# The decay matrix of a gated DeltaNet branch, with the constant triangle as stationary operand, in a one-core decoder layer

## The chip, the cores and the metric

The kernel runs on one core of one Trainium2 chip. The metric is device time in microseconds (us), median over runs. The core has a TensorE (PE in the profile; PEld is its loading of stationary operands), a VectorE (DVE), a ScalarE (ACT), a GpSimd (POOL) and a SyncE (SP), which issues all DMAs of this kernel.

## What is computed

One decoder layer over 512 positions of width 1024: three branches (differential attention with 8 heads, a gated DeltaNet with 8 heads, cross-attention into 256 memory tokens) read one normalised input through one wide projection, are gated, merged and projected; a squared-ReLU MLP follows. The change touches the DeltaNet branch, of which this much matters:

```python
g = -jnp.exp(dn_a_log[l]) * jax.nn.softplus(dn_a + dn_dt_bias[l])
G = jnp.cumsum(g, axis=-1)
decay = jnp.exp(jnp.where(causal, G[..., :, None] - G[..., None, :], -jnp.inf))
lower = jnp.where(strict, jnp.einsum('bhnid,bhnjd->bhnij', k_beta, k) * decay, 0.0)
intra = jnp.where(causal, jnp.einsum('bhnid,bhnjd->bhnij', q, k) * decay, 0.0)
```

The kernel works with chunks of 128 positions. For one head and chunk the exponent of the decay is a sum of g over the positions t that come after j and up to i. Written as a matrix product that is the sum over t of AFTER[t, j] * UPTO[t, i] * g[t], where AFTER and UPTO are constant 0/1 triangles. The g can be multiplied into either triangle before the product.

## The kernel before, in words

Two stages. The **mixing stage** (to about 760 us with the branches, to about 965 us with the last gate tiles and the merge) multiplies 104 tiles of weight columns with the normalised input. A tile is 128 columns of the combined projection; its product with all 512 positions goes to one of two PSUM banks (`acc`). Each float32 product is made of three fp32r products (L1866 to L1868: high by high, high by low, low by high), 8 x 3 matmuls of 512 columns for a tile. For each tile ScalarE casts the weights to their high part (L1066, `w_hi`), VectorE subtracts for the low part (L1388, `w_lo`), and ScalarE copies the finished bank out (`evac`). Three tiles of weights are held split ahead. The second stage (merge, output projection, MLP) is untouched by the change.

Between the eighths of the main tiles TensorE does the **side steps** of the branches, in a plan that `plan_order` makes when the kernel is built: a list of steps for each engine from a table of durations (`PE_US`, `ACT_US`, `DVE_US`, `POOL_US`), dependencies, and the order of the tiles in `ORDER`. The first 12 half tiles follow a table of their own (`first_order`). All engines work off their lists strictly in order; the plan decides places only, and semaphores hold the true dependencies.

The side steps of the DeltaNet run for four pairs of heads, p = 0 to 3, so 8 blocks (2 heads x 4 chunks) at a time, with results in `ps_d`, three PSUM banks that all these steps share:

- `dk` transposes k (L2009); ScalarE squares and copies it (L1209, L1210), VectorE makes the norms and `k_fac` (L1594 to L1601), GpSimd multiplies AFTER with the decays of 8 blocks into `d_ET` (L994).
- `dE` multiplies `d_ET` with UPTO, 8 float32 matmuls of 128 columns (L2016). ScalarE takes exp (L1207), GpSimd multiplies with `k_fac` (L999).
- `dq`, `dv` transpose q and v; VectorE writes V (L1604). `dL`, `dA` are the products of k with k and with q (L2051), multiplied by `d_ET` on VectorE (L1607, L1611).
- `T1`, `Za`, `Wb`, `Z5`, `W5`, `Zl`, `Wl` invert the triangular matrix with many 32x32 matmuls (L2023, L2027, L2029), `dU`, `dW`, `sa`, `sb`, `dO` apply it and carry the state.

The attention side steps are `av`, `as0`, `as1`, `at`, `ap`, `ay` for each head (L1970 to L1990). `as0` of head 0 is the first to use the bias strip, to which VectorE adds the causal mask (L1531).

The decays g themselves (`gdec`) come from VectorE's routine `beta_and_decay` (L1461 to L1483), which raises `g_ready`; the PE step `decay` (L2073) waits for it. In the list of VectorE a conv tile is four instructions (`conv`: L1493 and three of L1495), then ScalarE's tanh (L1155) and VectorE's product (L1510). A main tile t may start on TensorE when its low part is there (`lo_ready`) and tile t-2 is copied out (`acc_free`):

```python
if k0 == 0:
    pe.wait_ge(lo_ready, t + 1)
    pe.wait_ge(acc_free, t - 1)
```

In the stretch where the first `dE` stands, tiles 0 to 7 are `dk0 dk1 dq0 dq1 dv0 dv1 dz0 dz1`.

Of the kernel before, what the change touches and what calls it, by code (L numbers as in the profile page):

```python
# [23 lines left out]
F32R = mybir.dt.float32r  # L24
I32 = mybir.dt.int32
ALU = mybir.AluOpType
# [29 lines left out]
NCONST = 4 + NM  # L56

# [15 lines left out]
PE_US = {"dE": 1.79, "dL": 1.79, "dA": 1.79, "dU": 1.79, "dW": 1.79, "T1": 0.55, "Za": 0.55, "Wb": 1.05, "Z5": 0.55, "W5": 0.9, "Zl": 1.2, "Wl": 1.2, "sa": 0.45,  # L73
# [5 lines left out]
POOL_US = {"dk": 2.4, "dE": 2.4, "dL": 2.5, "dA": 5.8}  # L79
# [9 lines left out]
         ("gate", 1), ("head", 1), ("conv", 2), ("head", 2), ("gate", 1), ("z", 1), ("head", 3), ("gate", 2), ("z", 2),  # L89
         ("head", 4), ("gate", 2), ("conv", 3), ("head", 5), ("gate", 5), ("head", 6), ("head", 7), ("gate", 4),  # L90
         ("z", 3), ("gate", 9)]
# [335 lines left out]
def build(nc, weights, x, mem, w_ba, params, consts, onehot, relb, post_g, y_dram, gate_dram, f_dram, frep_dram, out):  # L427
# [18 lines left out]
    with ExitStack() as ctx:  # L446
# [17 lines left out]
        cst = sb("cst", [P, NCONST, P])  # L464
# [39 lines left out]
        names = ["U", "SCR", "K", "KB", "V", "TF", "XB", "ET", "LT", "AT", "TT"]  # L504
        B = {n: sd_("d_" + n, [P, 8, P]) for n in names}
        U, SCR, K, KB, V, TF, XB, ET, LT, AT, TT = (B[n] for n in names)
# [12 lines left out]
        eyes = cst[:, C_MASK0 + NM - 1, 0:QB]  # L519
# [180 lines left out]

        LAMS, LAME, NLAM = smd[:, 2:4], smd[:, 4:6], smd[:, 6:7]
# [143 lines left out]
        def _(sp):  # L845
# [25 lines left out]
            sp.dma_start(cst[:, C_ID + 1:], consts[:, C_ID + 1:]).then_inc(in_cst, 16)  # L871
# [103 lines left out]
        def _(pool):  # L975
# [8 lines left out]
            def delta(i):  # L984
# [5 lines left out]
                if kind == "dk":  # L990
                    pool.wait_ge(g_ready, 1)
                    if p:
                        pool.wait_ge(yb_out, 16 * p)
                    last = nc.gpsimd.tensor_tensor(ET[:], over(cst[:, C_AFTER, :], 8),  # L994
                                                   along(flat(gdec[:, heads]), P), ALU.mult)
# [365 lines left out]
        def _(dve):  # L1361
# [97 lines left out]
            def beta_and_decay():  # L1459
# [4 lines left out]
                dve.wait_ge(in_cst, 16)  # L1464
# [12 lines left out]
                for n in range(15, 1, -2):  # L1477
# [5 lines left out]
                V_.scalar_tensor_tensor(out=gdec[:], in0=ba[:, 1], scalar=-1.0, in1=along(ealog, ST),  # L1483
                                        op0=ALU.mult, op1=ALU.mult).then_inc(g_ready, 1)
# [34 lines left out]
            def attn(i):  # L1519
# [8 lines left out]
                else:  # L1528
                    if (kind, h) == ("as0", 0):
                        dve.wait_ge(strip_in, 16)  # L1530
                        link(V_.tensor_tensor(strip[:, :, P:2 * P], strip[:, :, P:2 * P],  # L1531
                                              over(cst[:, C_CAUS, :], HA), ALU.add))
# [271 lines left out]
        def _(pe):  # L1804
# [188 lines left out]
            def delta(i):  # L1993
# [20 lines left out]
                elif kind == "dE":  # L2014
                    for m in range(8):
                        last = mm(dst[m], ET[:, m], cst[:, C_UPTO, :], start=True, stop=True)  # L2016
# [50 lines left out]
            def decay():  # L2067

                pe.wait_ge(g_ready, 1)
                pe.wait_ge(in_cst, 16)  # L2070
# [286 lines left out]
```

## Time and profile before

| | |
|---|---|
| median of 3 runs | 1351.75 us (1351.54 to 1351.91) |
| profiled execution: time | 1350.3 us |
| profiled execution: span, first to last instruction | 1348.5 us |
| TensorE busy | 1322.5 us, 98% of the span |
| VectorE, ScalarE, GpSimd busy | 753.9, 470.9, 191.5 us |
| mean granted TensorE clock | 0.995 of full |

The profiled execution is one run with the profiler on; its own time is 1.8 us above its span. Busy times of TensorE count overlapping, pipelined matmuls once. A row of a timeline gives an instruction's start and its duration with pipeline fill; what a matmul costs in a stream is the distance between starts.

### The profile page before, as it was taken

How to read it: one execution, taken by the hardware profiler on the slowest of the kernel's cores; microseconds unless marked ns; L12 is line 12 of the kernel's file. 1: busy time of each engine (PE TensorE's matmuls, PEld its weight loads, DVE VectorE, ACT ScalarE, POOL GpSimd, SP SyncE). 2: the span in 40 equal slices, each digit the busy share in tenths (PEclk: the TensorE clock that was granted, in tenths of full speed). 3: DMA queues.
4: the chain of work that ended last, by engine and by line, in shares of the span. 5: the costliest groups of instructions: out<-in, count | busy, mean ns of one | idle time of the engine just before them, and what ended most of it. 6: DMA issues, size and time to landing. Idle time of an engine off the chain costs nothing.

```text
span 1348.5 us, 24282 instructions
## 1 busy us (share of the span) xinstructions
PE 1322.5 (98%) x10413; PEld 1111.1 (82%) x10413; DVE 753.9 (56%) x1289; ACT 470.9 (35%) x779; POOL 191.5 (14%) x136
## 2 busy tenths in 40 slices
PE   9899999999999999999999999999989999999997
PEld 8689987787788887888788888888988888888786
DVE  6885253675776675677447534554466522355335
ACT  5353424433443444334243421213443222222220
POOL 1113000012000130003101042233112200022000
PEclk9999999999999999999999999999999999999999
DMA  6064313232213222222213466654323333332311
GB/s 222 28 203 139 100 48 110 78 95 72 72 48 94 94 72 88 66 99 92 83 48 102 141 210 211 191 161 132 128 92 111 106 112 94 94 94 95 109 63 63
DMA packets 59458, 143.66 MB, mean 107 GB/s; under 512 B 5032, under 2 KB 23896, under 8 KB 59352
## 3 DMA queue, kind: packets, MB, share of 16 engines
q1 hardware_dynamic: 59352, 142.12, 32.7%
q8 instruction: 83, 1.36, 0.4%
q14 instruction: 23, 0.19, 0.0%
HBM read 127.40 MB, written 16.27 MB: 107 GB/s over the span
## 4 chain that ended last, share of the span: by engine, by line
PE 90%; DVE 6%; ACT 2%; issue 1%; DMA 1%; SPq 0%; DVEq 0%; ACTq 0%
PE acc L1866 18%; PE acc L1868 18%; PE acc L1867 18%; PE ps_a L1868 2%; PE ps_a L1866 2%; PE ps_a L1867 2%; PE ps_d L2051 2%; PE ps_a L1975 2%; PE ps_d L2184 2%; PE ps_a L2184 2%; PE ps_a L2186 2%; PE ps_d L2185 2%; PE ps_d L2186 2%; PE ps_a L2185 2%; PE ps_a L1986 1%
## 5 line engine op out<-in xcount | busy, mean ns | idle before, releaser
L1388 DVE TENSOR_TENSOR w_lo<-w_raw,w_hi 128x1024 fp32r<-128x1024 f32 x172 | 232.7, 1354 | 205.0 <-ACT w_hi L1066 204.0
L1066 ACT CAST w_hi<-w_raw 128x1024 fp32r<-128x1024 f32 x172 | 180.3, 1048 | 414.8 <-PE acc L1868 344.7
L1866 PE MATMUL acc<-n_hi,w_hi 128*128 128x512 f32 (+1 forms) x776 | 313.2, 404 | 2.1 <-ACT conv_x L1141 1.6
L1868 PE MATMUL acc<-n_hi,w_lo 128*128 128x512 f32 (+1 forms) x776 | 300.1, 387 | 0.7 <-issue 0.7
L1867 PE MATMUL acc<-n_lo,w_hi 128*128 128x512 f32 (+1 forms) x776 | 300.0, 387 | 0.0
L1866 PEld LDWEIGHTS acc<-n_hi,w_hi 128*128 128x128 f32 x776 | 146.4, 189 | 32.5 <-issue 4.8
L1868 PEld LDWEIGHTS acc<-n_hi,w_lo 128*128 128x128 f32 x776 | 146.2, 188 | 30.3
L1867 PEld LDWEIGHTS acc<-n_lo,w_hi 128*128 128x128 f32 x776 | 146.6, 189 | 25.9 <-issue 0.7
L1868 PE MATMUL acc<-y_hi,w_lo 128*128 128x512 f32 x192 | 74.7, 389 | 0.0
L1866 PE MATMUL acc<-y_hi,w_hi 128*128 128x512 f32 x192 | 74.7, 389 | 0.0
L1867 PE MATMUL acc<-y_lo,w_hi 128*128 128x512 f32 x192 | 74.7, 389 | 0.0
L1054 POOL TENSOR_TENSOR h_lo<-sq,h_hi 128x512 fp32r<-128x512 f32 x32 | 41.4, 1294 | 234.2 <-DVE h_hi L1782 234.2
L1388 DVE TENSOR_TENSOR wx_lo<-w_raw,wx_hi 128x1024 fp32r<-128x1024 f32 x28 | 43.5, 1557 | 52.8 <-ACT wx_hi L1066 52.7
L1023 POOL TENSOR_SCALAR gate_st<-gate_st 128x512 f32<-128x512 f32 x24 | 23.6, 985 | 319.1 <-ACT gate_st L1148 319.1
L1321 ACT ACTIVATE sq<-relu 128x512 f32<-128x512 f32 x32 | 20.2, 632 | 116.2 <-DVE relu L1780 116.2
L1495 DVE SCALAR_TENSOR_TENSOR conv_y<-conv_x,par,conv_y 128x512 f32<-128x512 f32 x72 | 57.7, 801 | 2.6
L994 POOL TENSOR_TENSOR d_ET<-cst,gdec 128x1024 f32<-128x1024 f32 x4 | 8.4, 2088 | 266.4 <-PE ps_d L2009 198.2
L1066 ACT CAST wx_hi<-w_raw 128x1024 fp32r<-128x1024 f32 x28 | 29.2, 1043 | 44.0 <-PE acc L2186 30.7
L1868 PEld LDWEIGHTS acc<-y_hi,w_lo 128*128 128x128 f32 x192 | 36.0, 188 | 7.5
L1867 PEld LDWEIGHTS acc<-y_lo,w_hi 128*128 128x128 f32 x192 | 36.0, 188 | 7.5
L1866 PEld LDWEIGHTS acc<-y_hi,w_hi 128*128 128x128 f32 x192 | 36.0, 188 | 7.4
L1866 PE MATMUL acc<-m_hi,w_hi 128*128 128x256 f32 x128 | 37.3, 292 | 0.0
(401 smaller groups left out, 2512.1 us busy)
## 6 DMA issues: line engine op xcount, KB each, us to landing
w_raw<-weights SPq DMA_DIRECT2D x200, 512.0 KB, 3.5
gate_scratch<-gate_st SPq DMA_DIRECT2D x24, 256.0 KB, 2.8
g_in<-gate_scratch SPq DMA_DIRECT2D x24, 256.0 KB, 3.9
y_raw<-y_scratch SPq DMA_DIRECT2D x16, 256.0 KB, 3.7
x_tok<-x SPq DMA_DIRECT2D x4, 512.0 KB, 5.2
y_scratch<-y_st SPq DMA_DIRECT2D x4, 512.0 KB, 2.6
y_scratch<-d_ET SPq DMA_DIRECT2D x4, 512.0 KB, 3.4
y_scratch<-y_st SPq DMA_DIRECT2D x8, 256.0 KB, 2.4
```

Source lines behind the costliest of these rows:

```text
L1054: nc.gpsimd.tensor_tensor(h_lo[:, f % 16], sq[:, f % 2], h_hi[:, f % 16].bitcast(F32), ALU.subtract).then_inc(hl_ok, 1)
L1066: nc.scalar.copy(hi_of_tile(t), w_raw[:, t % RAW]).then_inc(hi_ready, 1)
L1388: V_.tensor_tensor(lo_of_tile(t), w_raw[:, t % RAW], hi_of_tile(t).bitcast(F32), ALU.subtract).then_inc(lo_ready, 1)
L1495: ins = V_.scalar_tensor_tensor(out=y, in0=conv_x[:, n % 2, j:j + S], scalar=par[:, col + j:col + j + 1], in1=y, op0=ALU.mult, op1=ALU.add)
L1866: mm(bank, wh, hi_of(k), start=start and k == 0, stop=False)
L1867: mm(bank, wh, lo_of(k), start=False, stop=False)
L1868: last = mm(bank, wl, hi_of(k), start=False, stop=stop and k == KT - 1)
L1975: last = mm(ps[:, col:col + (q + 1) * P], qkv_T[rows_m, h % 2, 0, q * P:(q + 1) * P], qkv_T[rows_m, h % 2, 1, 0:(q + 1) * P], start=True, ...
L2051: last = mm(dst[m], a[:, m], b[:, m], start=True, stop=True)
L2184: mm(to, high, wh, start=kb == 0, stop=False)
L2185: mm(to, low, wh, start=False, stop=False)
L2186: return mm(to, high, wl, start=False, stop=kb == 2 * KT - 1)
```

## The change

It does four things.

1. The decays are multiplied into UPTO instead of AFTER, and they are split in a high part rounded to fp32r and a rest (`g_parts`, kept in the columns of `par` that held the lambda vectors). GpSimd's step `dk` is now two multiplications of 128x1024, into `sums_hi` and `sums_lo` (fp32r). These two lie in the memory of `d_ET` and `d_AT`.
2. `dE` has AFTER (`after_r`, an fp32r copy) as stationary operand and the sums moving, in 512 columns: 4 matmuls in place of 8 of float32.
3. VectorE's routine for the decays has three more instructions ahead of `g_ready`. The constants are loaded by two DMAs in place of one, without the masks that nothing read.
4. The plan is given 0.91 in place of 1.79 for `dE` on PE, 4.8 in place of 2.4 for `dk` on POOL, and a new `ORDER`: tiles dz4, dz5 now come ahead of gates 18, 19, and gates 3, 4 ahead of head 7.

```diff
-PE_US = {"dE": 1.79, "dL": 1.79, "dA": 1.79, "dU": 1.79, "dW": 1.79, "T1": 0.55, "Za": 0.55, "Wb": 1.05, "Z5": 0.55, "W5": 0.9, "Zl": 1.2, "Wl": 1.2, "sa": 0.45,
+PE_US = {"dE": 0.91, "dL": 1.79, "dA": 1.79, "dU": 1.79, "dW": 1.79, "T1": 0.55, "Za": 0.55, "Wb": 1.05, "Z5": 0.55, "W5": 0.9, "Zl": 1.2, "Wl": 1.2, "sa": 0.45,
...
-POOL_US = {"dk": 2.4, "dE": 2.4, "dL": 2.5, "dA": 5.8}
+POOL_US = {"dk": 4.8, "dE": 2.4, "dL": 2.5, "dA": 5.8}
...
-         ("gate", 1), ("head", 1), ("conv", 2), ("head", 2), ("gate", 1), ("z", 1), ("head", 3), ("gate", 2), ("z", 2),
-         ("head", 4), ("gate", 2), ("conv", 3), ("head", 5), ("gate", 5), ("head", 6), ("head", 7), ("gate", 4),
-         ("z", 3), ("gate", 9)]
+         ("gate", 1), ("head", 1), ("conv", 2), ("head", 2), ("gate", 1), ("z", 1), ("head", 3), ("z", 2),
+         ("gate", 2), ("head", 4), ("gate", 2), ("conv", 3), ("head", 5), ("gate", 5), ("head", 6), ("gate", 2),
+         ("head", 7), ("z", 3), ("gate", 11)]
...
-            sp.dma_start(cst[:, C_ID + 1:], consts[:, C_ID + 1:]).then_inc(in_cst, 16)
+            sp.dma_start(cst[:, C_ID + 1:S_EYES], consts[:, C_ID + 1:S_EYES]).then_inc(in_cst, 16)
+            sp.dma_start(cst[:, S_CAUS], consts[:, C_CAUS]).then_inc(in_cst, 16)
...
-                    last = nc.gpsimd.tensor_tensor(ET[:], over(cst[:, C_AFTER, :], 8),
-                                                   along(flat(gdec[:, heads]), P), ALU.mult)
+                    g_hi, g_lo = (g_parts[:, n, 8 * p:8 * p + 8] for n in range(2))
+                    nc.gpsimd.tensor_tensor(sums_hi[:], over(cst[:, C_UPTO, :], 8), along(g_hi, P), ALU.mult)
+                    last = nc.gpsimd.tensor_tensor(sums_lo[:], over(cst[:, C_UPTO, :], 8), along(g_lo, P), ALU.mult)
...
-                V_.scalar_tensor_tensor(out=gdec[:], in0=ba[:, 1], scalar=-1.0, in1=along(ealog, ST),
-                                        op0=ALU.mult, op1=ALU.mult).then_inc(g_ready, 1)
+                link(V_.scalar_tensor_tensor(out=gdec[:], in0=ba[:, 1], scalar=-1.0, in1=along(ealog, ST),
+                                             op0=ALU.mult, op1=ALU.mult))
+                V_.tensor_copy(after_r[:], cst[:, C_AFTER, :])
+                link(V_.tensor_copy(g_parts[:, 0].bitcast(F32R), flat(gdec[:])))
+                V_.tensor_tensor(g_parts[:, 1], flat(gdec[:]), g_parts[:, 0], ALU.subtract).then_inc(g_ready, 1)
...
                 elif kind == "dE":
-                    for m in range(8):
-                        last = mm(dst[m], ET[:, m], cst[:, C_UPTO, :], start=True, stop=True)
+                    for n in range(2):
+                        for part in (sums_hi, sums_lo):
+                            last = mm(ps_d[:, n], after_r[:], part[:, 4 * n:4 * n + 4].rearrange("p a b -> p (a b)"),
+                                      start=part is sums_hi, stop=part is sums_lo)
...
-                pe.wait_ge(in_cst, 16)
+                pe.wait_ge(in_cst, 32)
```

What the plan makes of it, at three places. In the changed kernel the lines L1866 to L1868 are L1879 to L1881, L2016 is L2030, L1986 is L1999, and L2023, L2027, L2029 are L2038, L2042, L2044.

TensorE around the first `dE`, before (a wait for `acc_free` and `lo_ready` marks the start of a main tile, here of dz1):

```order
190 L1867 MATMUL acc<-n_lo,w_hi 128x512
191 L1868 MATMUL acc<-n_hi,w_lo 128x512
192 L2016 MATMUL ps_d<-cst,d_ET 128x128 [waits d_pool,d_act]
193 L2016 MATMUL ps_d<-cst,d_ET 128x128 x7
194 L1866 MATMUL acc<-n_hi,w_hi 128x512 [waits acc_free,lo_ready]
195 L1867 MATMUL acc<-n_lo,w_hi 128x512
```

and of the change, the start of dz1 and then the step:

```order
190 L1880 MATMUL acc<-n_lo,w_hi 128x512
191 L1881 MATMUL acc<-n_hi,w_lo 128x512
192 L1879 MATMUL acc<-n_hi,w_hi 128x512 [waits acc_free,lo_ready]
193 L1880 MATMUL acc<-n_lo,w_hi 128x512
194 L1881 MATMUL acc<-n_hi,w_lo 128x512
```

```order
202 L1880 MATMUL acc<-n_lo,w_hi 128x512
203 L1881 MATMUL acc<-n_hi,w_lo 128x512
204 L2030 MATMUL ps_d<-sums_hi,after_r 128x512 [waits d_pool,d_act]
205 L2030 MATMUL ps_d<-sums_lo,after_r 128x512
206 L2030 MATMUL ps_d<-sums_hi,after_r 128x512
207 L2030 MATMUL ps_d<-sums_lo,after_r 128x512
208 L1879 MATMUL acc<-n_hi,w_hi 128x512
```

The first half of dz1 (12 matmuls) now stands ahead of `dE`; the second half and then `dq` follow. `dE` of pairs 1, 2 and 3 too stands one to two eighths of a tile later than before.

VectorE at the end of the routine for the decays, before (L1388 is the low part of the next weight tile, L1493 the next conv):

```order
88 L1481 TENSOR_SCALAR ba<-ba 128x32 [waits vch]
89 L1482 SCALAR_TENSOR_TENSOR ba<-ba 128x32 [waits vch]
90 L1483 SCALAR_TENSOR_TENSOR gdec<-ba,sml 128x32 [waits vch]
91 L1388 TENSOR_TENSOR w_lo<-w_raw,w_hi 128x1024 [waits hi_ready]
92 L1493 TENSOR_SCALAR conv_y<-conv_x,par 128x512 [waits acc_free]
```

and of the change:

```order
90 L1493 SCALAR_TENSOR_TENSOR gdec<-ba,sml 128x32 [waits vch]
91 L1495 CAST after_r<-cst 128x128 [waits vch]
92 L1496 CAST par<-gdec 128x32
93 L1497 TENSOR_TENSOR par<-gdec,par 128x32 [waits vch]
94 L1398 TENSOR_TENSOR w_lo<-w_raw,w_hi 128x1024 [waits hi_ready]
```

`g_ready` is raised by the last of the three new rows instead of by the `gdec` row.

TensorE in the inversion of pair 3, before (`Za` L2023, `ap` of head 5 L1986, `Wb` L2027 and L2029):

```order
2561 L1868 MATMUL acc<-n_hi,w_lo 128x512
2562 L2023 MATMUL ps_d<-d_TT,d_SCR 32x32 [waits d_pool,d_dve,d_act]
2563 L2023 MATMUL ps_d<-d_TT,d_SCR 32x32 x31
2564 L1986 MATMUL ps_a<-v_tok,wT 128x128 [waits a_dve,a_act]
2565 L1986 MATMUL ps_a<-v_tok,wT 128x128 x9
2566 L2027 MATMUL ps_d<-d_TT,d_XB 32x32 [waits d_dve,d_act]
2567 L2027 MATMUL ps_d<-d_TT,d_XB 32x32 x3
2568 L2029 MATMUL ps_d<-d_XB,d_TT 32x32 x4
```

and of the change:

```order
2576 L1999 MATMUL ps_a<-v_tok,wT 128x128 [waits a_dve,a_act]
2577 L1999 MATMUL ps_a<-v_tok,wT 128x128 x9
2578 L2038 MATMUL ps_d<-d_TT,d_SCR 32x32 [waits d_pool,d_dve,d_act]
2579 L2038 MATMUL ps_d<-d_TT,d_SCR 32x32 x31
2580 L1879 MATMUL acc<-n_hi,w_hi 128x512
2581 L1880 MATMUL acc<-n_lo,w_hi 128x512
```

The three steps stood back to back; now two eighths of main work (12 matmuls) stand between `Za` and `Wb`. From `dE` of pair 3 to `dO` of pair 3 nearly every side step stands elsewhere among the main tiles. Up to `dk` of pair 1 nothing but the places of the first `dE` and `dq` changes.

## Rows read from the trace of the kernel before

**Rows 1.** The page: busy times, and the chain that ended last by engine.

```profile
PE 1322.5 (98%) x10413; PEld 1111.1 (82%) x10413; DVE 753.9 (56%) x1289; ACT 470.9 (35%) x779; POOL 191.5 (14%) x136
...
PE 90%; DVE 6%; ACT 2%; issue 1%; DMA 1%; SPq 0%; DVEq 0%; ACTq 0%
```

**Rows 2.** TensorE's waits: line <- releaser: us in total, times, longest.

```profile
PE ps_d L2016 <- ACT d_K L1210: 3.0, 1, 3.0
PE ps_d L2073 <- DVE gdec L1483: 2.8, 1, 2.8
PE ps_d L2027 <- DVE d_XB L1614: 1.8, 1, 1.8
...
PE ps_d L2029 <- issue: 0.9, 1, 0.9
```

**Rows 3.** Timeline of TensorE, second and third `dE`: start, us, what.

```profile
266.02 1.95 PE L2016 MATMUL ps_d<-cst,d_ET 128*128 128x128 f32 x16
267.72 0.48 PE L1866 MATMUL acc<-n_hi,w_hi 128*128 128x512 f32 x1
...
457.39 0.48 PE L1866 MATMUL acc<-n_hi,w_hi 128*128 128x512 f32 x1
457.71 0.40 PE L1867 MATMUL acc<-n_lo,w_hi 128*128 128x512 f32 x1
```

**Rows 4.** Timeline of TensorE around the first `dE`.

```profile
73.54 0.39 PE L1867 MATMUL acc<-n_lo,w_hi 128*128 128x512 f32 x1
73.77 0.39 PE L1868 MATMUL acc<-n_hi,w_lo 128*128 128x512 f32 x1
77.14 3.48 PE L2016 MATMUL ps_d<-cst,d_ET 128*128 128x128 f32 x16 [2.99 <-ACT d_K L1210]
80.39 0.47 PE L1866 MATMUL acc<-n_hi,w_hi 128*128 128x512 f32 x1
...
83.24 1.04 PE L2009 MATMUL ps_d<-cst,conv_qk 128*128 128x128 f32 x8
```

**Rows 5.** Stretch of the first `dE`: us, busy PE, PEld, DVE, ACT, POOL, granted clock, DMA.

```profile
77.20:80.40 3.20, 3.20 (x17) 3.20 (x17) 3.16 (x4) 2.88 (x4) 0.00 (x0) 0.53 0.57 204
```

**Rows 6.** Timeline of ScalarE, VectorE and GpSimd, 63 to 76 us.

```profile
63.92 2.33 DVE L1495 SCALAR_TENSOR_TENSOR conv_y<-conv_x,par,conv_y 128x512 f32<-128x512 f32 x3
...
70.11 2.42 POOL L994 TENSOR_TENSOR d_ET<-cst,gdec 128x1024 f32<-128x1024 f32 x1 [16.85 <-PE ps_d L2009]
...
74.66 0.60 ACT L1141 COPY conv_x<-acc 128x512 f32<-128x512 f32 x1
...
76.04 1.05 ACT L1210 COPY d_K<-ps_d 128x1024 f32<-128x1024 f32 x1
```

**Rows 7.** Timeline of VectorE alone, the conv tile beside GpSimd's L994.

```profile
70.81 3.06 DVE L1495 SCALAR_TENSOR_TENSOR conv_y<-conv_x,par,conv_y 128x512 f32<-128x512 f32 x2
70.81 2.27 DVE L1495 SCALAR_TENSOR_TENSOR conv_y<-conv_x,par,conv_y 128x512 f32<-128x512 f32 x1
```

**Rows 8.** Timeline beside two GpSimd instructions in a row.

```profile
47.99 5.27 POOL L982 TENSOR_TENSOR m_lo<-full,m_hi 128x1024 fp32r<-128x1024 f32 x2 [22.52 <-ACT m_hi L1080]
...
51.04 2.77 DVE L1495 SCALAR_TENSOR_TENSOR conv_y<-conv_x,par,conv_y 128x512 f32<-128x512 f32 x1
```

**Rows 9.** Timeline of VectorE: end of the routine for the decays, and a cast of 128x128.

```profile
62.15 0.19 DVE L1483 SCALAR_TENSOR_TENSOR gdec<-ba,sml 128x32 f32<-128x32 f32 x1
...
27.61 0.21 DVE L1442 CAST wb_hi<-w_ba_sb 128x128 fp32r<-128x128 f32 x1
```

**Rows 10.** Timeline: VectorE at `dv` and TensorE at `dL` of pair 0.

```profile
90.79 1.22 DVE L1604 TENSOR_TENSOR d_V<-ps_d,k_fac 128x1024 f32<-128x1024 f32 x1 [0.70 <-PE ps_d L2009]
...
93.47 1.95 PE L2051 MATMUL ps_d<-conv_qk 128*128 128x128 f32 x16
```

**Rows 11.** Timeline of TensorE, `Wb` of pair 3.

```profile
641.44 0.26 PE L2027 MATMUL ps_d<-d_TT,d_XB 32*32 32x32 f32 x8
...
643.58 0.26 PE L2029 MATMUL ps_d<-d_XB,d_TT 32*32 32x32 f32 x8 [0.92 <-issue]
```

More of the change, by code:

```diff
@@ L56 @@
 NCONST = 4 + NM
+S_EYES, S_CAUS = 8, 9
 PC_PRE, PC_MEM, PC_FF = 0, 8, 16
@@ L463, in build @@
         w_lo = sb("w_lo", [P, SPL, KT, P], F32R)
-        cst = sb("cst", [P, NCONST, P])
+        cst = sb("cst", [P, S_CAUS + 1, P])
+        after_r = sb("after_r", [P, P], F32R)
         ones = sb("ones", [P, P])
@@ L503, in build @@
         sd_ = sb_in(dl)
-        names = ["U", "SCR", "K", "KB", "V", "TF", "XB", "ET", "LT", "AT", "TT"]
+        names = ["U", "SCR", "K", "KB", "V", "TF", "XB", "LT", "TT"]
         B = {n: sd_("d_" + n, [P, 8, P]) for n in names}
-        U, SCR, K, KB, V, TF, XB, ET, LT, AT, TT = (B[n] for n in names)
+        U, SCR, K, KB, V, TF, XB, LT, TT = (B[n] for n in names)
+        c1 = ExitStack()
+        sc_ = sb_in(c1)
+        ET, AT = sc_("d_ET", [P, 8, P]), sc_("d_AT", [P, 8, P])
+        c1.close()
+        sums_hi, sums_lo = sd_("sums_hi", [P, 8, P], F32R), sd_("sums_lo", [P, 8, P], F32R)
         WT, O = SCR, LT
@@ L518, in build @@
         Y6 = part_of(SCR, 2, P // 2)
-        eyes = cst[:, C_MASK0 + NM - 1, 0:QB]
+        eyes = cst[:, S_EYES, 0:QB]
         c1 = ExitStack()
@@ L698, in build @@
         block = ctx.enter_context(nc.Block())
+        g_parts = par[:, PC_LAM:PC_LAM + 2 * HB * ST].rearrange("p (a b) -> p a b", a=2)
         LAMS, LAME, NLAM = smd[:, 2:4], smd[:, 4:6], smd[:, 6:7]
@@ L1463, in beta_and_decay @@
                 link(V_.tensor_scalar(NLAM, NLAM, LAM_INIT, None, ALU.subtract))
-                dve.wait_ge(in_cst, 16)
+                dve.wait_ge(in_cst, 32)
                 for q in range(1, 4):
@@ L1531, in attn @@
                         link(V_.tensor_tensor(strip[:, :, P:2 * P], strip[:, :, P:2 * P],
-                                              over(cst[:, C_CAUS, :], HA), ALU.add))
+                                              over(cst[:, S_CAUS, :], HA), ALU.add))
                     ps = flat(ps_a[:])
```

## The prediction

> **What bounds the kernel.** I read the page first. TensorE is busy for 98% of the span, and 90% of the chain that ended last is TensorE [rows 1]. So only two things change the time: TensorE work that goes or comes, and TensorE's waits. The list of its waits comes next: three long ones, 3.0 us at the first `dE`, 2.8 us at `decay`, 1.8 us at `Wb` of pair 1, and one of 0.9 us put down to issue [rows 2]. All lie in stages that the change touches. Then come the timelines around `dE` [rows 3, 4], the granted clock there [rows 5], and what the other engines did while TensorE waited [rows 6 to 10]. About 0.2% (2.7 us) is what a measurement of this kernel can tell from no change.
>
> **`dE` of pairs 1, 2 and 3: -2.45 us.** A `dE` is 8 float32 matmuls that show as 16 records. From its start to the start of the next main matmul it takes 267.72 - 266.02 = 1.70 us [rows 3]; the one of pair 2 is alike, that of pair 3 a little longer (1.81). Together 5.21 us. The new `dE` is 4 matmuls of 512 columns with fp32r operands, of the same kind as a main matmul, which costs the distance of two starts, 73.77 - 73.54 = 0.23 us [rows 4]. That makes 0.92 us, three times 2.76. The stationary operand is the same in all four, but the main stream loads one for each matmul at this pace too, so I take nothing off. The bound on the other side is 0.32 us for one of the four, which is what a first main matmul costs after a side step, 457.71 - 457.39 [rows 3].
>
> The rate is the place for a rule. The trace shows 0.23 us for a 512-column matmul in a dense stream. The Trainium skill, "TensorE: Matmul & The Clock Gate", section "Back-to-back issue gap", gives a sustained 131 ns for N=512 in a real kernel. By that figure each `dE` would be an estimated 0.4 us cheaper still, 1.2 us for the three. The same section also gives about 216 ns for an isolated gap, and the trace stands by that. I go by the row.
>
> **The decays come later: +0.65 us.** `decay` waits on TensorE for `gdec` (2.8 us), and VectorE runs there without a gap. Three instructions are put between. A chained one of 32 columns takes 0.19 us and about 0.03 us for the link; a cast of 128x128 takes 0.21 us [rows 9]. So 0.03 + 0.2 + 0.2 + 0.2 = about 0.65 us, all of it on TensorE's path. Everything behind it on VectorE and ScalarE shifts by the same, so I count it once. The second DMA of constants lands long before; it costs nothing, and if it were late, `decay` would wait for it.
>
> **The first pair: -0.95 us before that shift.** Before, the last matmul of dz0 was through at 74.0 us, TensorE stood until 77.14, `dE` took until 80.39, that is 3.25 us, and half of dz1 until 83.24 [rows 4]. The granted clock was 0.53 in that stretch, so TensorE ran at its lower level of 1.2 GHz after the idle stretch [rows 5]. Sum: 9.24 us.
>
> Now dz1 comes first. It does not wait for `d_K` (end 77.09) but for the copy of dv1 out of its bank, which ended at 75.26 [rows 6]. Taken alone this would leave a wait of 1.26 us. But that copy stands on ScalarE behind the tanh of dv0, and so behind VectorE's conv of dv0, and this conv runs beside GpSimd's `dk`. Here is what GpSimd did to it. Three L1495 take 2.33 us undisturbed [rows 6]. Beside L994 (70.11 to 72.53) the second took 2.27 us instead of 0.8, ending at 73.08, 0.55 us after GpSimd was done, and the third was undisturbed [rows 7]. With two GpSimd instructions in a row, a second VectorE instruction is caught as well: 51.04 to 53.81, again 0.55 us after GpSimd's end at 53.26 [rows 8]. So the new second multiplication (72.53 to 74.95, same length) catches the third L1495: it ends at about 75.5 instead of 73.87, 1.6 us later. The bounds are 0 (no catch) and 2.4 us, if GpSimd takes 2.63 us as in [rows 8] and also waits its turn for 0.5 us.
>
> The Trainium skill has the rule behind this, in "GPSIMD Engine Reference", section "8. Key points": GpSimd shares its SBUF interfaces with VectorE and contends with instructions that have two SBUF inputs. L1495 has two; the rows agree. It speaks against the change, which adds such GpSimd work.
>
> So the wait is 1.3 + 1.6 = 2.9 us, nearly as long as before, and I expect the low clock again behind it: +1.6 us, the price before (3.25 - 1.70). Then half of dz1 at 2.85 and `dE` at 0.92: 8.3 us in place of 9.24. `dE` itself should not wait: its `d_K` is late by the same 1.6 us (78.7) and TensorE gets there at about 79.8; GpSimd's sums are ready at 75. If that cover went, each us late would be a us of waiting.
>
> Behind this, VectorE's chain of pair 0 (norms, `k_fac`, V) is 1.6 us later against TensorE. V ended at 92.01 and `dL` began at 93.47 without a wait [rows 10]; that leaves nothing of the 1.46 us of margin, though the finish of dz1 (0.7 us) has moved behind V. I put **+0.2 us** there, between 0 and 1.
>
> **Pairs 1 to 3, the moves.** GpSimd's `dk` lasts 2 us longer for each, about 4 us, as the plan allows for: `dE` stands one or two eighths (1.4 us each) later, so no wait. VectorE is caught up to 2 us more in each, and hides it behind three split tiles ahead (16 us of main work). `Wb` of pair 1: its wait comes from VectorE, busy with the bias strip and the maxima of `as0`. It gets one more eighth of cover (+1.36), but VectorE now takes a w_lo (1.22 us) ahead of `Za`: the wait stays, **+0.1**. `Wb` of pair 3 stood right behind `Za` and `ap`, and its 64 small matmuls ran into an issue gap of 0.92 us [rows 11]; two eighths now stand between, and I take it as gone: **-0.9 us**. TensorE changes from main to side work 141 times instead of 139, at 0.09 us each (0.32 - 0.23): **+0.2**. [...]
>
> **Sum.** -2.45 + 0.65 - 0.95 + 0.2 + 0.1 - 0.9 + 0.2 = -3.15 us. The profiled execution's own 1350.3 us (span 1348.5) becomes 1347.15; it lies 1.45 us under the median of 1351.75, so the forecast for the median is **1348.6 us**.
>
> **Rivals.**
> *First: the first pair gets away warm.* If the third L1495 is not caught, or GpSimd's two instructions leave VectorE its turns, the wait is 1.3 to 2 us, and after so short a stand the clock may stay at its upper level. Then 1.3 + 2.85 + 0.92 = 5.1 us in place of 8.3: another 3.2 us at most, 1345.4; with the wait as forecast but no low clock, 1347.0. For it: the 1.3 us. Against: [rows 8].
> *Second: only the matmuls' saving is left and part is eaten.* The issue gap turns up elsewhere (+0.9; nothing says that it belongs to this place alone), and the first pair is at its bad bound (+0.8). 1348.6 + 1.7 = 1350.3 us, within 0.2%.
> *Third: slower.* The order of pair 3 is new from `dE` to `dO`, among two heads of attention, whose VectorE steps are long. At each hand-over from VectorE to TensorE there a wait like the one of 1.8 us [rows 2] can arise, where the plan's durations are short of the truth, GpSimd's catches being in none of them. Each costs 1.8. One or two only eat the gain; from four on (+7.2) the kernel is slower by over 0.2%: 1355.8 us. Against it: before, the plan had one such wait in four pairs.
> *That the new `dE` is not cheaper*, because the float32 product's real price is hidden under something, has nothing for it: TensorE has no gap around it.
>
> **Chances.** The forecast 0.50 (its spread straddles the bound of 1349.05: 0.33 faster, 0.17 within); first rival 0.17, faster; second 0.24, within; third 0.09, slower. So faster 0.50, same 0.41, slower 0.09. The range: down to 1345.6, the first rival nearly whole; up to 1352.0, which takes in the bad bounds of the first pair, of `dL` and one new wait of 1.8 us (1348.6 + 0.8 + 0.8 + 1.8). About 0.1 is left out above it and less below.
>
> **What the new profile would show.** `dE` from start to next start 0.92 us; GpSimd's `dk` as two rows of about 2 us; `decay` waiting 3.4 us; the wait of 3.0 us gone from `dE` and one of about 2.9 us at the first matmul of dz1, its releaser the copy out of the bank, with low clock behind it; one L1495 more of over 2 us; the 0.92 us of issue gone. I would be wrong if dz1 starts without a wait, or if new waits on VectorE stand in pair 3.

## The result, and the profile after

Over 18 runs of each on one chip the changed kernel took 1354.02 us (median; 1351.59 to 1357.64) and the kernel before 1351.53 us: ratio 1.002 [1.0013, 1.0027]. The change costs 2.5 us where 2.9 us of gain were forecast (1351.53 - 1348.6), and the result is outside the range. The profiled execution took 1352.0 us, with a span of 1350.2 us at a mean granted clock of 0.994; it stands 2.0 us under the median, so its rows are those of a good execution. The runs of some kernels below spread more widely (up to 10 us), so the intervals have to be read, not the medians alone.

The page of the changed kernel, busy times and the chain that ended last by engine, against [rows 1]:

```profile
PE 1321.0 (98%) x10365; PEld 1107.6 (82%) x10365; DVE 756.0 (56%) x1292; ACT 470.0 (35%) x779; POOL 199.4 (15%) x140
PE 87%; DVE 8%; ACT 2%; issue 2%; DMA 1%; SPq 0%; DVEq 0%; ACTq 0%
```

48 records of TensorE are gone, as they should be (four `dE`, 16 records to 4), and the same number of weight loads. Yet TensorE's share of the chain fell by three points, and VectorE and issue took them. The list of TensorE's waits, which answers to [rows 2]:

```profile
PE ps_d L2088 <- DVE par L1497: 3.3, 1, 3.3
PE ps_a L1988 <- issue: 2.4, 1, 2.4
PE acc L1879 <- ACT conv_x L1151: 1.8, 2, 1.5
PE ps_d L2022 <- DVE conv_v L1523: 1.3, 1, 1.3
PE acc L1879 <- issue: 1.2, 1, 1.2
PE ps_d L2044 <- issue: 1.2, 2, 0.7
...
PE ps_d L2042 <- DVE d_XB L1627: 0.7, 1, 0.7
PE ps_d L2022 <- ACT d_ET L1217: 0.6, 1, 0.6
```

Three things are to be seen. `decay` waits longer, as forecast (3.3 for 2.8 us). `Wb` of pair 1 waits 0.7 us in place of 1.8. And "issue", where TensorE waits for nothing that the profile shows, has grown to three rows of 4.8 us together, where it had one row of 0.9 in [rows 2] and two more, of 0.7 and 0.4 us, in the full list. The largest is a single gap of 2.4 us at a step of attention (`as`), which the change does not touch. The timeline of TensorE there:

```profile
529.07 1.30 PE L1988 MATMUL ps_a<-qkv_T 64*128 64x384 f32 x8 [2.44 <-issue]
530.30 0.79 PE L1879 MATMUL acc<-n_hi,w_hi 128*128 128x512 f32 x1
530.89 0.63 PE L1880 MATMUL acc<-n_lo,w_hi 128*128 128x512 f32 x1
531.32 0.63 PE L1881 MATMUL acc<-n_hi,w_lo 128*128 128x512 f32 x1
```

Behind the gap a main matmul costs the distance of two starts, 0.43 us (531.32 - 530.89), where 0.23 us is usual: the clock has fallen too. The table of stretches shows it, and the same behind `decay` (columns as in [rows 5]):

```profile
62.00:69.00 7.00, 5.87 (x17) 4.90 (x18) 5.42 (x12) 2.00 (x4) 0.00 (x0) 0.51 0.00 1
...
529.00:534.00 5.00, 4.93 (x19) 3.89 (x19) 3.21 (x8) 0.69 (x1) 0.00 (x0) 0.66 0.01 3
```

The granted clock is 0.51 from 62 to 69 us, from the end of the wait at `decay` on (59.8 to 63.1); this is the 1.2 GHz level. In the second stretch it is 0.66 on average, since the low level holds for 3.4 of the 5 us, from 529.7. A stretch of that length at 0.43 for 0.23 us a matmul costs 3.4 x (1 - 0.23/0.43) = 1.6 to 1.7 us.

**Where the 1.7 us between the spans come from** (1348.5 to 1350.2). Gaps of TensorE, from its first to its last matmul: 17.3 us before, 20.5 after, +3.2 (of that +2.5 between 160 and 960 us). Low clock ahead of the last 10 us: 6.8 us before, 10.2 after, about +1.7. Work: three `dE` at -0.8 each and the first, now at full clock, -0.8, with the switches +0.2: -3.0. Sum +1.9. So the matmuls' saving came, and gaps with what hangs on them ate it.

### The profile page after: what moved, and what is told of

It is laid out like the page before. It is cut to its first block, busy times and chain, and to the rows that moved or that the text cites. A ratio compares the mean times of both kernels' runs of the same rounds, so it can differ in the third digit from the quotient of the medians.

```text
span 1350.2 us, 24194 instructions
## 1 busy us (share of the span) xinstructions
PE 1321.0 (98%) x10365; PEld 1107.6 (82%) x10365; DVE 756.0 (56%) x1292; ACT 470.0 (35%) x779; POOL 199.4 (15%) x140
## 4 chain that ended last, share of the span: by engine, by line
PE 87%; DVE 8%; ACT 2%; issue 2%; DMA 1%; SPq 0%; DVEq 0%; ACTq 0%
PE acc L1879 18%; PE acc L1881 17%; PE acc L1880 17%; PE ps_a L1881 2%; PE ps_a L1880 2%; PE ps_a L1879 2%; PE ps_d L2066 2%; PE ps_a L1988 2%; PE ps_d L2199 2%; PE ps_a L2199 2%; PE ps_a L2200 2%; PE ps_d L2201 2%; PE ps_d L2200 2%; PE ps_a L2201 2%; PE ps_a L1999 1%
## 5 line engine op out<-in xcount | busy, mean ns | idle before, releaser
L1398 DVE TENSOR_TENSOR w_lo<-w_raw,w_hi 128x1024 fp32r<-128x1024 f32 x172 | 226.3, 1317 | 206.2 <-ACT w_hi L1076 205.4
L1879 PE MATMUL acc<-n_hi,w_hi 128*128 128x512 f32 (+1 forms) x776 | 314.0, 405 | 3.5 <-ACT conv_x L1151 1.8
L1881 PE MATMUL acc<-n_hi,w_lo 128*128 128x512 f32 (+1 forms) x776 | 300.9, 388 | 0.0
L1879 PEld LDWEIGHTS acc<-n_hi,w_hi 128*128 128x128 f32 x776 | 147.0, 189 | 32.7 <-issue 4.8
L1881 PEld LDWEIGHTS acc<-n_hi,w_lo 128*128 128x128 f32 x776 | 146.6, 189 | 30.4
L1879 PE MATMUL acc<-y_hi,w_hi 128*128 128x512 f32 x192 | 74.7, 389 | 0.0
L1881 PE MATMUL acc<-y_hi,w_lo 128*128 128x512 f32 x192 | 74.7, 389 | 0.0
L1004 POOL TENSOR_TENSOR sums_hi<-cst,par 128x1024 fp32r<-128x1024 f32 x4 | 8.2, 2041 | 268.7 <-PE ps_d L2022 199.5
L1879 PEld LDWEIGHTS acc<-y_hi,w_hi 128*128 128x128 f32 x192 | 36.0, 188 | 7.5
L1881 PEld LDWEIGHTS acc<-y_hi,w_lo 128*128 128x128 f32 x192 | 36.0, 188 | 7.4
L1879 PE MATMUL acc<-m_hi,w_hi 128*128 128x256 f32 x128 | 37.4, 292 | 0.0
```

What stands on the lines that cost most here:

```text
L1398: V_.tensor_tensor(lo_of_tile(t), w_raw[:, t % RAW], hi_of_tile(t).bitcast(F32), ALU.subtract).then_inc(lo_ready, 1)
L1879: mm(bank, wh, hi_of(k), start=start and k == 0, stop=False)
L1881: last = mm(bank, wl, hi_of(k), start=False, stop=stop and k == KT - 1)
```

## The experiments

**1. The same kernel once more.** Is the gap near 530 us (it begins between 526 and 532 us in the runs below) the kernel's or that execution's?

> The changed kernel once more, for a second profile of it. Theory 'decay wait' (the three new VectorE instructions lengthen TensorE's wait at decay from 2.76 to 3.3 us, and the low clock behind it lasts twice as long, 6.8 us for 3.4, which costs 1.7 us): both stand again at the same place, with the same lengths. Theory 'issue gaps' (TensorE stood 5.1 us for nothing but its own instructions against 2.0 before, one gap of 2.4 us with a low clock behind it): if the gaps belong to the new order they stand at the same places, near 315, 498, 529, 669 us; if they come by chance, they lie elsewhere and their sum is anything from 2 to 6 us. Time by both 1354, ratio to the kernel before 1.002.

Measured: 1353.95 us over 12 runs, ratio 1.0015 [1.0006, 1.0025]. The gaps came again: TensorE's waits between 160 and 700 us.

```profile
PE ps_a L1988 <- issue: 2.2, 1, 2.2
PE ps_d L2044 <- issue: 1.7, 2, 1.2
PE acc L1879 <- issue: 1.1, 1, 1.1
```

So they belong to the program, though the small ones vary: the one at 498 us is 1.2 us here and 0.6 above. What TensorE had before the gap is dense: `Wb` of pair 2, 64 matmuls of 32x32, then this `as`. The DMA view has a queue of its own for instructions, 82 transfers of 16 KB in the whole run, one for some 250 of TensorE's records (matmuls and loads). First the stretch of 517 to 527 us, then that of 527 to 529:

```profile
DMA packets 107, 0.37 MB, mean 37 GB/s; under 512 B 16, under 2 KB 16, under 8 KB 107
q1 hardware_dynamic: 107, 0.37, 15.6%
...
q8 instruction: 1, 0.02, 2.9%
```

The two rows above the dots are the first stretch, which holds all but the end of `Wb` (525.9 to 527.2 us): the instruction queue moved nothing there (it has no row). Its transfers stand at 515.6 and 527.9 us; 476 of TensorE's records went by between them, about twice the usual, and TensorE stands still from 528.0 to 530.2. So it stops as the transfer begins. This is the picture of an engine that has run out of instructions and waits for the next block. The long interval alone does not make a gap: 455 records went by ahead of the transfer at 337.7 us, and TensorE did not stand there.

**2. The plan alone.** The arithmetic of the kernel before, with the new `ORDER` and the new durations for the plan.

```diff
 # before.py with
-PE_US = {"dE": 1.79, ...
+PE_US = {"dE": 0.91, ...
-POOL_US = {"dk": 2.4, ...
+POOL_US = {"dk": 4.8, ...
 # and the ORDER of the change
```

> The kernel before (its float32 dE, its one GpSimd multiplication) with the plan of the change: the new ORDER and the new durations, so every engine works off the same list as in the change. Theory 'issue gaps belong to the new order': slower than before by the 3 us of gaps and 1.7 us of clock, 1355 to 1356 us, ratio 1.003. Theory 'decay wait': the plan itself is neutral or a little better (the first dE behind half of dz1 takes most of the 3.0 us wait away), 1349 to 1351.5 us, ratio 0.998 to 1.000.

Measured: 1349.3 us (1346.91 to 1357.12, 12 runs), ratio 0.9987 [0.9972, 1.0003]; span 1345.3. The waits between 160 and 700 us:

```profile
PE ps_d L2027 <- DVE d_XB L1614: 0.7, 1, 0.7
PE ps_d L2027 <- issue: 0.4, 1, 0.4
PE ps_d L2023 <- DVE d_TT L1616: 0.2, 1, 0.2
```

The tile order brings nothing bad and no gap at 530. It may be worth about 2.5 us by itself (1351.8 of the kernel before, run beside it, to 1349.3), but the interval reaches over 1, and three of the 12 runs lie 7 us or more above the fastest. Whatever made the change slower comes with the arithmetic, yet the gaps are far from its instructions.

**3. The arithmetic alone.** The change with the order and durations of before.

```diff
-PE_US = {"dE": 0.91, ...
+PE_US = {"dE": 1.79, ...
-POOL_US = {"dk": 4.8, ...
+POOL_US = {"dk": 2.4, ...
-         ... ("conv", 2), ("head", 2), ("gate", 1), ("z", 1), ("head", 3), ("z", 2),
+         ... ("conv", 2), ("head", 2), ("gate", 1), ("z", 1), ("head", 3), ("gate", 2), ("z", 2),
...
```

> The change's arithmetic (split decays, 4 matmuls of 512 columns, two GpSimd multiplications, three VectorE instructions) under the old plan: old ORDER, old durations 1.79 and 2.4. Theory 'issue gaps belong to the new order': the gaps are those of before, about 2 us; dE gives back 3.4 us, decay takes 0.55 to 2.2: 1349 to 1351 us, ratio 0.998 to 0.9995. Theory 'decay wait' with gaps by chance: 1351 to 1353 us; in the first pair dE stands ahead of dz1 again, waits for d_K about 3 us or more, with low clock. A mechanism that both share: dE of pairs 1 to 3 stands 4.1 us behind dk and GpSimd needs about 4.1 us, so up to 0.5 us of wait for each.

Measured: 1356.5 us, ratio 1.0039 [1.0025, 1.0053], above what either theory allowed. Two waits stand out, the first in 50 to 150 us, the second in 160 to 700 us:

```profile
PE ps_d L2030 <- ACT d_K L1220: 4.5, 1, 4.5
...
PE ps_a L1988 <- issue: 2.5, 1, 2.5
```

The first is the old place of the first `dE`, directly behind dz0: the wait of 3.0 us [rows 2] has become 4.5. The three conv instructions ahead of it take 5.36 us beside GpSimd's two multiplications, where they took 3.84 beside one in the kernel before. VectorE there, in the kernel before and in this one:

```profile
70.02 3.84 DVE L1495 SCALAR_TENSOR_TENSOR conv_y<-conv_x,par,conv_y 128x512 f32<-128x512 f32 x3
...
70.56 5.36 DVE L1508 SCALAR_TENSOR_TENSOR conv_y<-conv_x,par,conv_y 128x512 f32<-128x512 f32 x3
```

So the move of the first `dE` was right, and needed. The second is the gap at 530 again, under the old order. The two comparisons agree on the plan: -2.5 us with the old arithmetic (1349.3 against 1351.8) and with the new (1354.0 against 1356.5), each with an interval of some 4 us.

**4. `decay` ready earlier.** The first theory was that the three new instructions ahead of `decay` cost more than forecast, by the longer low clock behind it. Here `gdec` itself releases TensorE.

```diff
-                    pool.wait_ge(g_ready, 1)
+                    pool.wait_ge(g_ready, 2)
...
-                link(V_.scalar_tensor_tensor(out=gdec[:], in0=ba[:, 1], scalar=-1.0, in1=along(ealog, ST),
-                                             op0=ALU.mult, op1=ALU.mult))
+                V_.scalar_tensor_tensor(out=gdec[:], in0=ba[:, 1], scalar=-1.0, in1=along(ealog, ST),
+                                        op0=ALU.mult, op1=ALU.mult).then_inc(g_ready, 1)
                 V_.tensor_copy(after_r[:], cst[:, C_AFTER, :])
+                dve.wait_ge(g_ready, 1)
```

> The change, with the signal for the decays raised by the gdec instruction itself, as before; the three new instructions (cast of AFTER, split of the decays) come behind it, and only GpSimd waits for them. Theory 'decay wait': TensorE waits 2.8 us again at decay, the low clock behind it is back to 3.4 us, and the kernel gains 0.55 + 1.7 = 2.2 us on the change, 1351.8 us, ratio to before 1.000. Rival 'issue gaps': at most the 0.55 us come back, 1353.5 us, ratio 1.0015; the low clock behind decay is 6.8 us again in this profile or was chance.

Measured: 1353.44 us, ratio 1.0015 [1.0005, 1.0024]; span 1351.2. The wait at `decay` is 2.7 us, as before the change, and the low clock behind it lasts 3.4 us, as the theory had it. But the 2.2 us did not come: the median is 0.5 us below that of run 1, less than the intervals can tell. What came in its place is a wait of 2.8 us at the first matmul of dz1, the longest of the three waits of this row (50 to 160 us):

```profile
PE acc L1880 <- ACT conv_x L1151: 4.6, 3, 2.8
```

So the wait at `decay` does not explain the loss. Nor do the three instructions explain the low clock of 6.8 us, which also stands in the plan alone, without them. The gap near 530 us is here too, 2.4 us long, and this time the granted clock does not fall behind it.

**5. The number of instructions.** The theory now: a block of instructions ends at a fixed number in TensorE's stream, the new `dE` is 24 records shorter, and that moves the ends of blocks into dense stretches. Six matmuls of 32x32 (24 records; a float32 one is two loads and two matmuls) behind each `dE` put all that follows back to its old number, with the new arithmetic and plan.

```diff
+            def pad(n):
+                for _ in range(n):
+                    mm(ps_d[0:32, 2, 480:512], ones[0:32, 0:32], ones[0:32, 0:32], start=True, stop=True)
...
                 last.then_inc(d_mm, 1)
+                if kind == "dE":
+                    pad(6)
```

> The change with six 32x32 matmuls on constants behind each dE (their result is not used). They put back the 24 TensorE records by which the new dE is shorter, so that from there on every instruction stands at the same number in TensorE's stream as in plan_only; they cost about 0.13 us each time. Theory 'stream position' (the profiles show that the instruction queue fetches a block about once in 256 TensorE records, and the gap at 530 us of the change lies where 476 records passed between two fetches: gaps of this kind arise where a fetch falls in a stretch of small matmuls, so they hang on an instruction's number in the stream): the gap near 530 us of 2.2 us and the low clock behind it are gone, idle between 160 and 960 us falls from 5.9 to about 1.5 us, time 1347 to 1349 us, ratio 0.997. Rival 'the new arithmetic' (something in the split or in the second GpSimd multiplication holds TensorE up): the gap stays, 1354 us, ratio 1.0015 or a little more.

Measured: 1348.53 us, ratio 0.9991 [0.9976, 1.0006]; span 1347.5. Waits between 160 and 700 us:

```profile
PE ps_d L2047 <- DVE d_XB L1627: 0.7, 1, 0.7
PE ps_d L2047 <- issue: 0.6, 1, 0.6
PE ps_d L2043 <- DVE d_TT L1629: 0.2, 1, 0.2
```

Added work made the kernel 5.5 us faster than the change, and there is no gap at 530. That its time is the forecast (1348.6) is in part luck: three of its 12 runs lie 7 us higher, and the interval is 4 us wide and reaches over 1.

**6. The same, elsewhere: a scan.** All pads stand in `decay`, ahead of its wait, where TensorE has time. Everything behind is shifted by 4 records a pad.

```diff
             def decay():
+                pad(16)
                 pe.wait_ge(g_ready, 1)
```

> The change with sixteen 32x32 matmuls on constants ahead of decay's wait, where TensorE stands 3.3 us anyway: everything behind has a number in the stream that is 64 records higher; nothing else changes. Theory 'stream position': the gaps between 160 and 960 us move to other steps and their sum changes, from 1 to 8 us, and the time with it by 2 us or more either way. Rival 'the new arithmetic' or chance: the same gaps at the same steps, 1354 us.

> As shift_64 with thirty-two matmuls, a shift of 128 records. Theory 'stream position': another set of gaps again, differing from both others, with a time of its own between 1347 and 1358 us. Rival: 1354 us, gaps where they were.

> The same with forty-eight matmuls, a shift of 192 records, the last quarter of the scan 0, 64, 128, 192. Theory 'stream position': its own set of gaps, time anywhere between 1345 and 1356 us and unlike that of shift_256. Rival 'awake': 1345 to 1347 us as shift_64 and shift_128.

> The change with sixty-four 32x32 matmuls on constants ahead of decay's wait: a shift of 256 records, one whole block. The control for shift_64 and shift_128. Theory 'stream position': modulo a block everything stands where it does in the change, so the gap of about 2.2 us near 530 us and the low clock behind it are back, idle between 160 and 960 us about 6 us, 1352 to 1354 us, ratio 1.001. Rival 'awake' (the matmuls in the wait keep TensorE busy, and that is what shift_64 and shift_128 gained by): no loss, 1345 to 1347 us, ratio 0.996.

| shift, records | 0 | 64 | 128 | 192 | 256 |
|---|---|---|---|---|---|
| pads | 0 | 16 | 32 | 48 | 64 |
| median, us | 1354.02 | 1345.21 | 1346.85 | 1351.45 | 1353.87 |
| ratio to before | 1.002 | 0.9954 [0.9942, 0.9966] | 0.9964 [0.9953, 0.9976] | 0.9999 [0.9988, 1.0009] | 1.0021 [1.0011, 1.003] |

Sixteen tiny matmuls take off 8.8 us; 64 give all of it back. The last is the control: with a shift of one whole block the time of the change returns, and with it the gap. It also speaks against the rival that the pads help by keeping TensorE busy in the wait at `decay`, as does the shift of 128, which is fast (1346.85) with 6.8 us of low clock behind `decay`. With 192 the gap near 530 is gone too, but one of 2.3 us stands at 112.6 us in `Wb` of pair 0, with 3.4 us of low clock behind it.

Not all of the 8.8 us are issue gaps. The spans of the two profiles differ by 6.0 us (1350.2 to 1344.2): TensorE's gaps between 160 and 960 us fall from 6.0 to 2.1, the low clock at 530 goes (1.7), and the first pair, where clock and waits both change, makes up the rest. The other 2.8 us of the medians stand in no profile; the change was profiled in one of its faster runs.

Waits of the kernel with 256, then of that with 64, between 160 and 700 us:

```profile
PE ps_a L1993 <- issue: 2.5, 1, 2.5
PE ps_d L2049 <- issue: 1.9, 2, 1.3
PE acc L1884 <- issue: 1.2, 1, 1.2
...
PE acc L1885 <- issue: 1.0, 1, 1.0
PE ps_d L2047 <- DVE d_XB L1627: 0.7, 1, 0.7
PE ps_d L2043 <- DVE d_TT L1629: 0.2, 1, 0.2
```

**7. The gap without the new arithmetic.** At `Wb` of pair 2 the change has had three `dE` and stands 72 records earlier than the plan alone. 184 records of pads put the plan alone at the same point of a block (256 - 72); 248 put it where the change with 64 stands.

```diff
 # plan alone, in decay()
+                pad(46)        # 62 in the second
```

> plan_only (the old arithmetic under the new plan) with forty-six 32x32 matmuls ahead of decay's wait, a shift of 184 records. The change is 72 records behind plan_only from the third dE to the fourth, and 184 is 256 less 72: so between 460 and 600 us this kernel has the stream position of the change, modulo a block of 256. Theory 'stream position': the gap of about 2.2 us near 528 us and the low clock behind it appear in a kernel without any of the new arithmetic; time 1352 to 1355 us. Rival 'the new arithmetic': no such gap, time as plan_only, 1349.3 us.

> The old arithmetic under the new plan with sixty-two matmuls, a shift of 248 records: from the third dE to the fourth it has the position of shift_64 (64 - 72 is 248 less 256). It prices the new arithmetic where no gap stands. Theory 'the saving of the matmuls is real' : slower than shift_64 (1345.2 us) by three dE and a bit, 1.5 to 3.5 us, 1346.7 to 1348.7 us. Rival 'the new arithmetic gives nothing': 1345.2 us or less. If another part of its stream (pair 3 has 24 records more) has a gap, idle between 160 and 960 us shows it and is taken off.

Measured with 184: 1354.25 us, ratio 1.0017 [1.0003, 1.0031]; with 248: 1348.41 us, ratio 0.9988 [0.9973, 1.0004]. The first has the gap, in the waits between 160 and 700 us, with 3.4 us of low clock behind it:

```profile
PE ps_a L1980 <- issue: 2.4, 1, 2.4
PE ps_d L2034 <- issue: 1.1, 1, 1.1
```

The second has none over 0.7 us. This is the strongest of the runs: old arithmetic, the same plan, and the gap of 2.4 us made to come by the number alone. The records between the two transfers around `Wb` of pair 2 agree: in each of the six profiles with the gap (the change twice, arithmetic alone, earlier release, shift of 256, this one) 476 records go by ahead of the transfer at the gap. In nine of the ten without it a transfer more stands at 519 to 522 us, and 318 to 324 records go by ahead of the next; the shift of 192 has 460 there and does not stand.

The 1354.25 us are not the price of this gap alone. The shift of 184 fits the change only from the third `dE` to the fourth; in pair 0 this kernel has a second gap, of 2.3 us at 111.7 us and with 3.4 us of low clock behind it, which the change has not (50 to 160 us):

```profile
PE ps_d L2034 <- issue: 2.9, 2, 2.3
```

**8. The kernel before, shifted.** Does 64 help there as well?

```diff
 # before.py, in decay()
+                pad(16)
```

> The kernel before, with sixteen such matmuls ahead of decay's wait, a shift of 64 records. Theory 'stream position': the gaps of before (0.4 us at 122, 0.7 at 313, 0.9 at 644 us) give way to others, and its time moves by 1 us or more from 1351.7, either way, 1348 to 1356 us. Rival: its time and gaps stay, 1351 to 1352 us.

Measured: 1350.45 us, ratio 0.9996 [0.9985, 1.0006]: no difference that can be told. The gaps moved only in part: those of 0.4 us at 122 and 0.7 at 313 us are gone and ones of 0.5 at 339 and 0.7 at 668 us have come, but the one at 643 us stayed (1.2 us). A shift is good or bad for one order of one program; it is no remedy in itself.

**9. The best again, and with the earlier release.** The first is the kernel with 64 records of shift, unchanged; the second adds the edit of run 4 to it.

```diff
 # the change, in decay()
+                pad(16)
 # in the second also, as in run 4
+                V_.scalar_tensor_tensor(out=gdec[:], ...).then_inc(g_ready, 1)
```

> The fastest kernel so far once more, beside other runs of the kernel before. Theory 'stream position': the gaps are set by the code, so its profile shows the same few gaps between 160 and 960 us (about 2 us in all, none above 1.1) and its time is 1345 to 1346.5 us again. Rival (the 1345.2 us were a good hour of the chip): 1348 us or more.

> shift_64 with the signal for the decays raised by the gdec instruction (as in early_ready). Theory: TensorE's wait at decay is 0.6 us shorter and nothing moves in the stream, so 0 to 0.6 us less than shift_64, 1344.6 to 1345.2 us; the wait at the first matmul of dz1 stays 2.8 us, since VectorE's conv of dv0 is caught twice by GpSimd as before. Rival: the shorter wait lets a low clock begin elsewhere and the time is as shift_64 or up to 1.7 us more.

The first: 1346.16 us, ratio 0.9954 [0.9941, 0.9967]; the gain of 0.5% over the kernel before holds, and it is the version that beats both. Its gap of 1.0 us at 352 us is down to 0.2 in this profile, so the small gaps are not the kernel's alone. The second: 1346.52 us, ratio 0.9975 [0.9958, 0.9992], with four of 12 runs 7 us higher: the earlier release adds nothing, though it shortens the wait at `decay` from 2.2 to 1.6 us. Its rival came true: 6.8 us of low clock stand behind `decay`, where the first has none, and the wait at dz1 is 0.4 us in place of 2.8.

## Why the prediction was wrong, point by point

**The failed step: the issue gaps.** The sum said of the gap at `Wb` of pair 3 "two eighths now stand between, and I take it as gone: -0.9 us", and the second rival priced the other way at "+0.9; nothing says that it belongs to this place alone". The gap at that place did go. But a gap belongs to a number in TensorE's stream and what stands there, not to a place in the order alone, and the change shortens the stream by 24 records at each `dE`. So all gaps behind were dealt anew: one of 1.2, one of 0.6, one of 2.4 and one of 0.7 us by the timeline where there had been 0.7 and 0.9, and low clock of 3.4 us behind the 2.4 (+1.7). In place of -0.9 stands about +5 between 160 and 960 us (gaps +3.6 beside `Wb` of pair 1, clock +1.7). Put the stream back and the time is 1348.5 (run 5). The rival had the mechanism and a small part of its price (0.9 of about 6.2). The list of waits before the change had held three issue gaps (0.4, 0.7, 0.9); the prediction priced one of them.

**`dE`, -2.45: right.** One timeline holds it: the starts of the first `dE`'s four matmuls and of the next main one.

```profile
78.97 0.39 PE L2030 MATMUL ps_d<-sums_hi,after_r 128*128 128x512 f32 x1
79.20 0.39 PE L2030 MATMUL ps_d<-sums_lo,after_r 128*128 128x512 f32 x1
79.42 0.39 PE L2030 MATMUL ps_d<-sums_hi,after_r 128*128 128x512 f32 x1
79.65 0.39 PE L2030 MATMUL ps_d<-sums_lo,after_r 128*128 128x512 f32 x1
79.88 0.39 PE L1879 MATMUL acc<-n_hi,w_hi 128*128 128x512 f32 x1
```

79.88 - 78.97 = 0.91 us, at 0.23 us each, against 1.70 in [rows 3]. The row was the right price and the 131 ns of the Trainium skill ("TensorE: Matmul & The Clock Gate", "Back-to-back issue gap") was not met; its 216 ns is near. What the new arithmetic is worth in the whole is not settled. The fairest pair, with the same numbers in the stream throughout, is pads behind `dE` against the plan alone: -0.8 us by the medians, +0.6 by the fastest runs (1347.5 against 1346.9). Shift 64 against plan with 248 gives -3.2 us (-1.9 by the fastest runs), and change against plan with 184 gives -0.2, but there the plan carries a gap of 2.3 us more. The interval of each ratio is 2 to 4 us wide.

**The decays, +0.65: right as a wait.** 3.31 against 2.76 us of wait is +0.55, and the earlier release brought it back to 2.7. What it costs in time is not shown: the medians of runs 1 and 4 differ by 0.5 us, less than the intervals can tell.

**The first pair, -0.95: the mechanism right, but not what took place in the change.** The forecast chain stands in the kernel with 64 records of shift, almost number for number. Its timeline of VectorE, GpSimd, ScalarE and TensorE:

```profile
70.62 5.37 DVE L1508 SCALAR_TENSOR_TENSOR conv_y<-conv_x,par,conv_y 128x512 f32<-128x512 f32 x3
...
70.71 2.42 POOL L1004 TENSOR_TENSOR sums_hi<-cst,par 128x1024 fp32r<-128x1024 f32 x1 [17.40 <-PE ps_d L2027]
73.09 2.35 POOL L1005 TENSOR_TENSOR sums_lo<-cst,par 128x1024 fp32r<-128x1024 f32 x1
...
76.78 0.60 ACT L1151 COPY conv_x<-acc 128x512 f32<-128x512 f32 x1
...
77.52 0.47 PE L1884 MATMUL acc<-n_hi,w_hi 128*128 128x512 f32 x1 [2.77 <-ACT conv_x L1151]
```

Three conv instructions take 5.37 us beside GpSimd in place of 2.33 [rows 6] and end 0.55 us behind it (75.99 against 75.44), the copy ends at 77.38 and TensorE waited 2.77 us (forecast 2.9). With one multiplication beside them, in the kernel before, the same three took 3.84 us: the catch of the third costs 1.5. In the changed kernel itself the wait was 0.3 us. The low clock behind `decay` held for 6.8 us there (in the kernel before 3.4); so GpSimd began 1.1 us later than in the timeline above (71.83) and caught less (3.85 us for the three), and TensorE reached dz1 late. The time came back as small waits at `dq`, `dv` and `dL`: 0.6, 1.3 and 0.3 us. With 0.3 that is 2.5 us against the forecast's 2.9 + 0.2. What I had not thought of is that the low clock itself can take the place of the wait. The other runs with this arithmetic and plan agree: where the low clock behind `decay` lasted 6.8 us (change, change again, shifts of 128 and 192, the last of run 9), the wait at dz1 was 0 to 0.4 us; where it lasted 3.4 us or did not come (earlier release, pads behind `dE`, shifts of 64 and 256), it was 2.3 to 2.8.

**`Wb` of pair 1, +0.1: wrong by -1.2.** The wait fell from 1.78 to 0.65 us; the eighth of cover counted, the w_lo ahead of `Za` did not. The same 0.65 stands with the plan alone, so it is the plan's doing, and part of its -2.5 us.

**The third rival, slower by new waits on VectorE in pair 3: did not come.** Behind 160 us and up to 960 us TensorE waits for VectorE only at `Wb` of pair 1 (0.65) and once for 0.2 us. The kernel was slower in another way. The 0.09 for slower was too low because issue gaps were priced by the one seen.

**Open.** That the gap moves with the number in the stream is shown by the shifts; that a late block is its cause is argued, from the count of records and the times of the transfers. Why the one at 528 us came so late, whether because of the weight loads beside it or because TensorE's buffer has only a fixed reach, was not tried. The weight loads alone do not make the gap: in the kernel with 64 records of shift they fill the same microseconds ahead of the transfer at 526.5 us, and TensorE does not stand. No shift of the kernel before but 64 was tried, so its own best may lie lower too. It is also open why the low clock behind `decay` lasts 6.8 us in some programs and 3.4 in others, and why two of the six gaps near 530 us had no low clock behind them. Nor is it known what the runs some 7 us above the rest are, which several kernels have: in four of these kernels (plan alone, pads behind `dE`, plan with 248, the last of run 9) the profile is that of an execution near the lowest time.

## What to carry to other kernels

The number of instructions ahead of a dense stretch of small matmuls is part of a change: a saving of 24 records far ahead can cost more than it brings. Before a change of less than 1% is judged, look for waits put down to issue, compare them in a second profile, and run the kernel with 64, 128 and 192 records of padding at a place where the engine waits anyway, both kernels of the comparison, with a shift of a whole block as the control. A gap of 2 to 3 us costs its length and, where the granted clock falls behind it for 3.4 us, about 1.7 us more; it does not fall behind every such gap.

## What the runs showed of the hardware

- The instruction queue moves 82 transfers of 16 KB in a run, one for about 256 of TensorE's records. In or behind dense 32x32 matmuls gaps of 1.0 to 2.5 us stand that move with the instruction's number in the stream and come back after a shift of 256 (1354.0, 1345.2, 1346.9, 1351.5, 1353.9 us for shifts of 0, 64, 128, 192, 256 records).
- Behind the gap of 2.44 us the granted clock went to the 1.2 GHz level for 3.4 us, from 529.7 us on, with no wait for another engine near it. [Rows 5] had shown this only behind a wait for another engine. Behind the gaps of 2.44 and 2.46 us in the kernels with the earlier release and with the arithmetic alone it did not fall.
- Two GpSimd instructions in a row held three VectorE instructions of 0.8 us back to 5.37 us, to 0.55 us behind GpSimd's own end. The same 0.55 had stood in [rows 7, 8]; with one GpSimd instruction the last of the three was free, and they took 3.84 us.
